# First mixer of a two-block network: the three queues in another order, pair sums on VectorE, fillers between the output products

## What is computed

```python
z = rmsnorm(h) @ w_in                    # split into hq, hf, hi, hg, cq, ckv, kr
# half A: gated recurrence, 4 heads of 128, in chunks of 64 tokens
log_f, k = gate(hf); q = silu(hq); b = cumsum(log_f)
att = (q_t * exp(b_t - b_s) * k_s), s <= t          # inside a chunk
o   = att @ v + (q * exp(b)) @ S;  S' = exp(b_last) * S + (k * exp(b_last - b))^T @ v
o_a = rmsnorm(o, out_gain) * silu(hg)
# half B: latent attention, 4 heads of 128 + 64 rotated
q, kv = rmsnorm(cq) @ w_q_up, rmsnorm(ckv) @ w_kv_up
o_b = softmax(rope(rmsnorm(q)) @ rope(rmsnorm(k))^T) @ v   # block causal
h  += concat(o_a, o_b) @ w_out
```

## Time and profile before

| | us |
|---|---|
| median of three runs | 1336.14 |
| the profiled execution | 1339.7 |
| its span | 1337.9 |
| first mixer, intra(0) to the first product of wout | 56.05 to 216.92 |
| TensorE busy in the span | 1290.3 (96%) |
| VectorE, ScalarE busy | 894.0 (67%), 740.4 (55%) |
| mean granted TensorE clock | 0.966 |

### The profile page before, as it was taken

How to read it: one execution, slowest core, us unless ns; L and a number is a source line. 1 busy time by engine, 2 the same in 40 slices (tenths; PEclk the granted TensorE clock), 3 DMA queues, 4 the chain that set the end, 5 groups by cost and what they waited for, 6 DMA issues and landing times.

```text
span 1337.9 us, 24797 instructions
## 1 busy us (share of the span) xinstructions
PE 1290.3 (96%) x10371; PEld 1264.1 (94%) x10371; DVE 894.0 (67%) x1546; ACT 740.4 (55%) x1263; POOL 7.6 (1%) x17
## 2 busy tenths in 40 slices
PE   5898999999999999999999999999999989999997
PEld 5888887999999999999999999999999989999997
DVE  4753537576544666644486599985687857999655
ACT  5742324466444566533455566664676766666544
POOL 1000000000000000000000000000000000000000
PEclk9988678999999999999999999999989999999998
DMA  6221104365555265555365365656355333666630
GB/s 243 85 84 43 48 17 142 113 218 175 189 172 165 94 209 183 187 188 183 121 226 188 104 203 192 191 186 219 99 158 191 127 126 127 194 200 191 205 127 32
DMA packets 58891, 205.54 MB, mean 154 GB/s; under 512 B 6515, under 2 KB 8860, under 8 KB 58524
## 3 DMA queue, kind: packets, MB, share of 16 engines
q1 hardware_dynamic: 57104, 201.77, 46.3%
q10 hardware_dynamic: 1676, 2.19, 0.5%
HBM read 202.87 MB, written 1.06 MB: 152 GB/s over the span
## 4 chain that ended last, share of the span: by engine, by line
PE 90%; DVE 4%; ACT 4%; DMA 1%; issue 1%; ACTq 0%; DVEq 0%
PE PS L361 69%; PE PS L409 7%; PE PS L372 2%; PE PS L447 2%; PE PS L630 1%; PE PS L392 1%; ACT WH L339 1%; DVE WL L346 1%; PE PS L496 1%; PE PS L2229 1%; ACT EE L2387 1%; PE PS L668 0%; ACT L508 0%; PE PS L667 0%; PE PS L826 0%
## 5 line engine op out<-in xcount | busy, mean ns | idle before, releaser
L346 DVE TENSOR_TENSOR WL<-RAW,WH 128x1024 fp32r<-128x1024 f32 (+2 forms) x385 | 460.3, 1201 | 219.9 <-ACT WH L339 219.3
L339 ACT ACTIVATE WH<-RAW 128x1024 fp32r<-128x1024 f32 (+2 forms) x385 | 392.3, 1038 | 235.5 <-PE PS L361 201.5
L361 PE MATMUL PS<-UH,WH 128*128 128x256 f32 (+2 forms) x1576 | 451.5, 286 | 14.3 <-DVE WL L346 7.6
L361 PE MATMUL PS<-UL,WH 128*128 128x256 f32 (+2 forms) x1576 | 451.1, 286 | 0.0
L361 PE MATMUL PS<-UH,WL 128*128 128x256 f32 (+2 forms) x1576 | 451.1, 286 | 0.0
L361 PEld LDWEIGHTS PS<-UH,WH 128*128 128x128 f32 (+1 forms) x1576 | 301.6, 191 | 16.1 <-DVE WL L346 8.4
L361 PEld LDWEIGHTS PS<-UH,WL 128*128 128x128 f32 (+1 forms) x1576 | 301.8, 191 | 0.0
L361 PEld LDWEIGHTS PS<-UL,WH 128*128 128x128 f32 (+1 forms) x1576 | 300.3, 191 | 0.0
L361 PE MATMUL PS<-HL,WH 128*128 128x272 f32 (+1 forms) x512 | 145.8, 285 | 0.0
L361 PE MATMUL PS<-HH,WH 128*128 128x272 f32 (+1 forms) x512 | 145.7, 285 | 0.0
L361 PE MATMUL PS<-HH,WL 128*128 128x272 f32 (+1 forms) x512 | 145.4, 284 | 0.0
(11 more groups left out here) (390 smaller groups left out, 1988.3 us busy)
## 6 DMA issues: line engine op xcount, KB each, us to landing
RAW<-wpack SPq DMA_DIRECT2D x363, 512.0 KB, 4.2
RAW<-wpack SPq DMA_DIRECT2D x16, 384.0 KB, 3.5
RAW<-wpack SPq DMA_DIRECT2D x6, 256.0 KB, 2.7
X<-xin SPq DMA_DIRECT2D x1, 1088.0 KB, 5.1
C<-cst SPq DMA_DIRECT2D x1, 1072.0 KB, 10.1
HB<-bias_rows ACTq DMA_DIRECT2D x1, 1024.0 KB, 5.3
out<-X SPq DMA_DIRECT2D x4, 256.0 KB, 2.3
VF<-cst ACTq DMA_DIRECT2D x1, 512.0 KB, 4.2
```

What stands on the lines that cost most here:

```text
L339: a.e.activation(WH[n % NH][:, 0:w], RAW[n % NR][:, 0:w], ACT.Copy).then_inc(*a.mark("wh", n))
L346: v.e.tensor_tensor(WL[n % NH][:, 0:w], RAW[n % NR][:, 0:w], WH[n % NH][:, 0:w].bitcast(f32), ALU.subtract).then_inc(*v.mark("wl", n))
L361: ins = t.e.matmul(o, part(n, hw, kw, a, b), x(kx), start=first and not i and not p, stop=last and i == len(kcs) - 1 and p == 2)
```

## The change

Every edit is in the first mixer and the norm ahead of it. On TensorE levels, sums, spreads, values, rotations and projections stand in another order; the recurrence's output products stand ahead of the scores, two fillers before them and two between heads. VectorE adds pairs of squares (latent_pairs, head_pairs) and TensorE sums one array in place of two. VectorE does operands ahead of the eviction of a level, exponents two levels ahead, and KD, QE earlier; ScalarE's list follows. Left out of the diff: the first norm's root sums take 16 columns in place of 128 for the 16-token block, with RS set to 1 by GpSimd at the start; two memsets of zeros go; queries on ScalarE is cut in two, its second part being query_rest.

```diff
...
 def latent_sums():
     b = banks.take(t, ("lat",), ("lm",))
+    t.wait_ge("lsum")
     for x in range(2):
-        for m in range(2):
-            t.wait_ge("lsq", 2 * x + m)
         for i, a in enumerate(WIDE):
-            for m in range(2):
-                ins = t.e.matmul(PS[:, b, 3 * x + i:3 * x + i + 1], LSQ[:, 2 * x + m, a:a + 128],
-                                 ONE[:, 0:1], start=m == 0, stop=m == 1)
+            ins = t.e.matmul(PS[:, b, 3 * x + i:3 * x + i + 1], LSQ[:, 2 * x, a:a + 128], ONE[:, 0:1],
+                             start=True, stop=True)
     ins.then_inc(*t.mark("mix", "lat"))
-def head_sums_by_token(key, sq, rsq, freed):
-    t.wait_ge("zero", 8)
-    t.wait_ge("hsq", key, 0)
-    t.wait_ge("hsq", key, 1)
+def head_sums_by_token(key, sq, freed):
+    t.wait_ge("hsum", key)
     b = banks.take(t, ("hs", key), freed)
     for i, a in enumerate(WIDE):
         for hh in range(4):
-            o = PS[:, b, 4 * i + hh:4 * i + hh + 1]
-            t.e.matmul(o, sq(hh)[:, a:a + 128], ONE[:, 0:1], start=True, stop=False)
-            ins = t.e.matmul(o, rsq(hh)[:, a:a + 128], ONE[:, 0:1], start=False, stop=True)
+            ins = t.e.matmul(PS[:, b, 4 * i + hh:4 * i + hh + 1], sq[:, hh, a:a + 128], ONE[:, 0:1],
+                             start=True, stop=True)
     ins.then_inc(*t.mark("mix", "hs", key))
...
 level(0)
 project("kr", (0,), "ev")
+level(1)
 latent_sums()
-level(1)
 up("qup", 0, [(0, 0), (1, 1)], 128, ("qn",))
+level(2)
 up("qup", 1, [(0, 0), (1, 1)], 64, ("gr", "q"))
-level(2)
+level(3)
+spread_columns("l", lambda i, hh, n: LAT[0:n, 1, i:i + 1], ("rkv",), 1)
 up("kvup", 0, [(0, 2), (1, 3)], 128, ("kn",))
-spread_columns("l", lambda i, hh, n: LAT[0:n, 1, i:i + 1], ("rkv",), 1)
+level(4)
 value_up()
-level(3)
+level(5)
+head_sums_by_token("q", QSQ, ("qm",))
 values(0)
-head_sums_by_token("q", lambda hh: QSQ[:, hh, :], lambda hh: TMA[:, hh, :], ("qm",))
-level(4)
-values(1)
-head_sums_by_token("k", lambda hh: KSQ[:, hh, :], lambda hh: ACC[1][:, 1, :], ("hroot", "k"))
-level(5)
+head_sums_by_token("k", KSQ, ("hroot", "k"))
 rotate("q", QR, 4)
-project("hg", range(2), "ev")
 rotate("k", KR, 1)
-spread_columns("k", lambda i, hh, n: KSC[0:n, i, hh:hh + 1], ("rope", "k"), 4)
 for i, (a, z) in enumerate(TILES):
     t.wait_ge("kdec")
...
     for hh in range(4):
         ins = t.e.transpose(PS[0:z - a, b, 128 * hh:128 * hh + 128], KD[:, hh, a:z], ID[:, :])
     ins.then_inc(*t.mark("mix", "kt", i))
-project("hg", range(2, 4), "ev")
+values(1)
+spread_columns("k", lambda i, hh, n: KSC[0:n, i, hh:hh + 1], ("rope", "k"), 4)
 for ch in range(4):
     chunk(ch)
-for i in (2, 1, 0):
-    scores(i)
+project("hg", range(2), "ev")
+keep_going(t, 2)
 ob = banks.take(t, ("out",), ("outa",), 4)
 t.wait_ge("att", 6)
 t.wait_ge("qe")
...
             s0 = a + 64 * cc
             ins = t.e.matmul(PS[:, b, s0:s0 + 64], STS[2 * i + cc][:, vs], QE[:, hh, s0:s0 + 64],
                              start=False, stop=cc == 1)
+    if hh < 3:
+        keep_going(t, 2, done=("ones",))
 ins.then_inc(*t.mark("mix", "out"))
+scores(2)
+scores(1)
+out_sums()
+scores(0)
+project("hg", range(2, 4), "ev")
+out_rows()
 turn(0)
 turn(1)
-out_sums()
 attend(0)
 turn(2)
 attend(1)
 turn(3)
-out_rows()
 attend(2)
 attend(3)
...
+exponents(2)
 latent(1, 1)
 act_split(a, 15)
-exponents(2)
+exponents(3)
...
+act_split(a, 16)
...
+exponents(4)
+queries()
 act_split(a, 17)
-exponents(3)
-queries()
+exponents(5)
+query_rest()
 a.wait_ge("mix", "hr", "l")
...
-exponents(4)
+a.wait_ge("kn")
+a.wait_ge("lm")
+a.e.activation(KSQ[:, :, :], KN[:, :, :], ACT.Square).then_inc(*a.mark("hsq", "k", 0))
 value_rows()
-a.wait_ge("kn")
...
-act_split(a, 21)
-exponents(5)
-values(0)
-act_split(a, 23)
...
 a.wait_ge("decay")
 a.e.activation(E[:, :, :], E[:, :, :], ACT.Exp).then_inc(*a.mark("edec"))
 a.e.activation(EL[:, :, 0:1], B[:, :, 15:16], ACT.Exp)
 a.e.activation(EL[:, :, 1:5], B[:, :, 79:T:64], ACT.Exp).then_inc(*a.mark("el"))
+act_split(a, 21)
 a.wait_ge("kdec")
 a.e.activation(E[:, :, :], B[:, :, :], ACT.Exp).then_inc(*a.mark("eb"))
+a.wait_ge("qm")
+a.e.activation(QSC[:, :, :], QSC[:, :, :], ACT.Sqrt, bias=EPS[:, 0:1], scale=1.0 / 192).then_inc(
+    *a.mark("hroot", "q"))
+act_split(a, 22)
+values(0)
+act_split(a, 23)
+a.wait_ge("mix", "hs", "k")
+a.e.activation(KSC[:, :, :], PS[:, banks.at["hs", "k"], 0:12].rearrange("p (i h) -> p i h", h=4), ACT.Sqrt,
+               bias=EPS[:, 0:1], scale=1.0 / 192).then_inc(*a.mark("hroot", "k"))
...
+act_split(a, 25)
+values(1)
 act_split(a, 27)
-for h in range(4):
+for h in range(2):
     a.wait_ge("ev", "hg", h)
     a.e.activation(HG[:, h, :], HG[:, h, :], ACT.Silu).then_inc(*a.mark("hgsilu", h))
+a.wait_ge("mix", "out")
+a.wait_ge("qe")
+ob = banks.at["out",]
+a.e.activation(E[:, :, :], PS[:, ob:ob + 4, 0:T], ACT.Square).then_inc(*a.mark("osq"))
 preload(a, ACT.Exp)
 for i in (2, 1, 0):
     m, P = TILES[i][1] - TILES[i][0], (PM, PA, PB)[i]
...
                              scale=QSC[0:m, i, hh:hh + 1],
                              accum_out=STT[0:m, i, 4 + hh:5 + hh])
     ins.then_inc(*a.mark("pexp", i))
-a.wait_ge("mix", "out")
-a.wait_ge("qe")
-ob = banks.at["out",]
-a.e.activation(E[:, :, :], PS[:, ob:ob + 4, 0:T], ACT.Square).then_inc(*a.mark("osq"))
+a.wait_ge("mix", "hs", "o")
+a.e.activation(ROOTO, PS[:, banks.at["hs", "o"], 0:T], ACT.Sqrt, bias=EPS[:, 0:1], scale=1.0 / 128).then_inc(
+    *a.mark("hroot", "o"))
+for h in range(2, 4):
+    a.wait_ge("ev", "hg", h)
+    a.e.activation(HG[:, h, :], HG[:, h, :], ACT.Silu).then_inc(*a.mark("hgsilu", h))
...
-a.wait_ge("mix", "hs", "o")
-a.e.activation(ROOTO, PS[:, banks.at["hs", "o"], 0:T], ACT.Sqrt, bias=EPS[:, 0:1], scale=1.0 / 128).then_inc(
-    *a.mark("hroot", "o"))
+a.wait_ge("onorm")
+a.e.activation(UH[:, 0:4, :], OUTA[:, :, :], ACT.Copy).then_inc(*a.mark("uh", "o", 3))
 attend(0)
 turn(2)
 attend(1)
 turn(3)
-a.wait_ge("onorm")
-a.e.activation(UH[:, 0:4, :], OUTA[:, :, :], ACT.Copy).then_inc(*a.mark("uh", "o", 3))
 attend(2)
 attend(3)
...
+def latent_pairs():
+    for m in range(4):
+        v.wait_ge("lsq", m)
+    l4 = LSQ[:, :, :].rearrange("p (x m) t -> p x m t", x=2)
+    v.e.tensor_tensor(l4[:, :, 0, :], l4[:, :, 0, :], l4[:, :, 1, :], ALU.add).then_inc(*v.mark("lsum"))
+def head_pairs(key, sq, rsq):
+    v.wait_ge("hsq", key, 0)
+    v.wait_ge(*(("hsq", "q", 1) if key == "q" else ("krsq",)))
+    v.e.tensor_tensor(sq[0:64, :, :], sq[0:64, :, :], rsq, ALU.add).then_inc(*v.mark("hsum", key))
...
-    v.wait_ge(*(("mix", "hs", "q") if key == "q" else ("rsum", "q")))
+    v.wait_ge(*(("hsum", "q") if key == "q" else ("rsum", "q")))
...
-prepare(0)
-attention(0)
+exponents(1)
+operands(0)
 latent(0, 0)
 latent(0, 1)
+attention(0)
+exponents(2)
 dve_split(v, 13)
+latent(1, 0)
+operands(1)
 attention(1)
-prepare(1)
-latent(1, 0)
+exponents(3)
 latent(1, 1)
+latent_pairs()
+dve_split(v, 14)
 key_rest()
-dve_split(v, 14)
+operands(2)
+attention(2)
 latent_means()
+exponents(4)
 dve_split(v, 15)
-attention(2)
-prepare(2)
+operands(3)
+attention(3)
 latent_roots()
-dve_split(v, 17)
+exponents(5)
+dve_split(v, 16)
+operands(4)
+attention(4)
 query_rest()
-attention(3)
-prepare(3)
-keys()
-v.wait_ge("krsq")
-v.e.tensor_scalar(KR[:, 0, :], KR[:, 0, :], g("krn", 0, 64), None, ALU.mult).then_inc(*v.mark("gr", "k"))
-dve_split(v, 19)
-query_means()
-attention(4)
-prepare(4)
-dve_split(v, 21)
-query_roots()
-attention(5)
-prepare(5)
-key_roots()
-dve_split(v, 23)
-rotated("q", QR[:, :, :], 4)
-attention(6)
-v.wait_ge("op", 5)
+v.wait_ge("op", 4)
 v.e.tensor_tensor(E[:, :, 0:16], B[:, :, 15:16].to_broadcast([128, 4, 16]), B[:, :, 0:16], ALU.subtract)
 for hh in range(4):
     v4 = (lambda z: z[:, hh, 16:T].rearrange("p (n s) -> p n s", s=64))
     ins = v.e.tensor_tensor(v4(E), v4(B)[:, :, 63:64].to_broadcast([128, 4, 64]), v4(B), ALU.subtract)
 ins.then_inc(*v.mark("decay"))
+dve_split(v, 17)
+keys()
+operands(5)
+attention(5)
+head_pairs("q", QSQ, QRSQ)
+dve_split(v, 18)
+attention(6)
+head_pairs("k", KSQ, KRSQ.unsqueeze(1).to_broadcast([64, 4, T]))
+v.e.tensor_scalar(KR[:, 0, :], KR[:, 0, :], g("krn", 0, 64), None, ALU.mult).then_inc(*v.mark("gr", "k"))
+dve_split(v, 19)
+query_means()
+v.wait_ge("edec")
+v.wait_ge("mix", "att", 0)
+v.wait_ge("op", 5)
+v.e.tensor_tensor(KD[:, :, :], K[:, :, :], E[:, :, :], ALU.mult).then_inc(*v.mark("kdec"))
+dve_split(v, 21)
+v.wait_ge("eb")
+v.e.tensor_tensor(QE[:, :, :], Q[:, :, :], E[:, :, :], ALU.mult).then_inc(*v.mark("qe"))
+query_roots()
+dve_split(v, 23)
+key_roots()
+rotated("q", QR[:, :, :], 4)
+rotated("k", KR[:, :, :], 1)
+normed()
+v.wait_ge("mix", "att", 6)
+chunk(0)
+for ch in range(1, 4):
+    chunk(ch)
+dve_split(v, 25)
 divided("hg", 0, HG)
 divided("hg", 1, HG)
-rotated("k", KR[:, :, :], 1)
-v.wait_ge("edec")
-v.wait_ge("mix", "att", 0)
-v.e.tensor_tensor(KD[:, :, :], K[:, :, :], E[:, :, :], ALU.mult).then_inc(*v.mark("kdec"))
-normed()
-dve_split(v, 25)
-v.wait_ge("eb")
```

(35 more changed lines are left out.)

32 lines of the change are left out of this document (8 added, 24 removed).

## The result

| | before | after |
|---|---|---|
| median, us | 1336.54 (4 runs, 1331.01 to 1337.06) | 1321.69 (4 runs, 1320.31 to 1322.67) |
| profiled execution, span | 1339.7, 1337.9 | 1322.67, 1320.9 |
| first product of wout starts | 216.92 | 197.18 |
| clock from 63.43 to that product | 0.77 | 0.82 |

The ratio is 0.9897, 95% interval 0.987 to 0.9925: faster by 1.0%, 14.9 us. The forecast was 1310.0 with a range of 1300 to 1321. The sign is right; the time is 11.7 us above the forecast and outside the range.

A forecast was written before the change was run, and what follows sets the result against it. TensorE was taken to bound the stretch from 63.43 us to wout, losing 18.0 us idle and 71 us at half clock. Stage by stage wout moved from 216.9 to 190.8, saving 26.1: 1336.1 − 26.1 = 1310.0 us, range 1300 to 1321.

The forecast's parts named there:

- 63.43 to kvup0: From the end of level(0)'s products: kr's wait gone, a new 3.2 us wait for QR, kvup0 at 86.0 instead of 89.43.
- kvup0 to the output: From 86.0 to 147.5: kvup0 at half clock (5.4), values(0) 8.5 plus 1.0, spread of k 4.5, chunks 3.7.
- The output: The recurrence's output products behind hg 0 and 1: full clock, 6.6 us, with six fillers 7.4, against 13.25 before.
- Scores and sums: Behind a new 2.4 us wait for OUTA: scores(2) 6.5, scores(1) 3.0, output sums 3.0, scores(0) 0.7 us.
- Four attends and two turns at the pace of before 7.5: Behind a 2.2 us wait for onorm, ahead of wout: these items take 7.5 us; UH, UL, WL 2.0 more.
- Everything behind it unchanged, about 1121 us: From the start of wout to the end: nothing changes, about 1121 us.
- B: Rival: the recurrence's output stays at half clock, 7.4 us longer, total 1317; chance 0.16.
- C: Rival: the clock stays up wherever TensorE is not long idle, total 1300; chance 0.13.
- D: Rival: the order only moves the waits, idle and half clock stay at 18 and 61 us, total 1330.5; chance 0.09.
- the sum by kinds: Cross-check of the saving: sums 6.7 less, fillers 1.1 more, idle 18.0 to 13.1, half clock 14: 24.5 us.
- E: Rival: slower, the fallen clock never rises from 86 to 181 us, some 52 us more, total 1362; chance 0.04.
- it falls everywhere and the output stays at half: Upper end of the terms, clock falling at all new waits: +7.4, values +2, the rest +4, total 1323.

The follow-up runs named there:

- third experiment: The changed kernel without its 8 fillers, the two ahead of the output and the six within it: 1317.87 us, ratio 0.9879.
- the version with fillers: The changed kernel with query_rest ahead of operands(4) and fillers ahead of KD's transposes, scores(2), attend(0) and wout: 1302.58 us, ratio 0.9763.

## Why the prediction was wrong

By its own steps, from the start of intra(0) (56.05 before, 54.63 after) to the start of wout: forecast a saving of 26.1 us, measured 160.87 − 142.55 = 18.3.

- **63.43 to kvup0: right.** kr without a wait and at full clock (3.14 us), 12 passes for the latents (1.47), a wait of 3.5 for QR, kvup0 at 84.96 (forecast 86.0; it would be 86.4 if intra(0) hadn't started 1.4 us earlier). The earlier start is not the change's doing: the changed kernel's own two traces differ by 1.0 us in it.
- **kvup0 to the output: right within 3.3 us, to the good.** kvup0 took 4.6 instead of 5.4, values(0) 8.6 at 1.00 where 1.0 was added for a fall, spread 3.8, chunks 3.3. The output started 88.2 us behind intra(0), forecast 91.45.
- **The output: right.** Full clock, 8.1 us for 7.4. The step "it follows 6 us of projections, so I take full clock" held; the term for the fillers was small, but the trace without them shows them as pure cost.
- **Scores and sums: mis-sized.** Forecast 6.5 + 3.0 + 3.0 + 0.7 = 13.2, measured 16.8. The step wrote that the clock falls again at the wait and then took the middle between full and half; it is at half throughout, 7.9 + 4.4 + 3.9.
- **"Four attends and two turns at the pace of before 7.5": the step that failed.** It priced them by the full-clock rate with a wait of 2.2 us written right ahead of them. They took 13.8. The forecast's own rule for kvup0 and for scores(2), a wait of this length is followed by half clock, was left out for the wait for onorm, and again for the one ahead of wout. With UH, UL and WL this is 15.95 us against 9.5. With 16 fillers in the wait the same items took 7.6 us, so it is the clock, and not the hand-offs between the engines, that the step had wrong.
- **"Everything behind it unchanged, about 1121 us" was off by 2.7 us:** 1123.7. The step took the diff's end for the change's end. The rotation of the banks carries the change on through all later layers, which the text did not look for. The longer wait for M, 1.6 us, is shown to come from it. Another 1.9 us lie behind that wait, where the changed kernel runs at half clock for a while and the kernel before does not (255.0 us to the end, against 253.1); their cause is open, and 0.8 came back on the way there.
- **Median and trace.** The spans differ by 17.0 us, the medians by 14.9: the profiled execution of before was 3 us above its median, that of the changed kernel 1.

Sum: 26.1 − 18.3 = 7.8, less 1.4 for the earlier start of intra(0), plus 2.7 and 2.1, is 11.2 of the 11.7 missed. The rest is the median of before, 1336.5 with a fourth run where the forecast had 1336.1.

**The rivals.** B falls (third experiment). C, the clock stays up, falls as a forecast for this kernel (2 × 0.18 × 133.75 = 48 us at half), but it is what the fillers make true, and its 1300 is near the 1302.3 that was then measured. D, only the waits move, got 0.09 and comes closest in sense: beside the pair sums the order brings 1 us, not to be told from nothing. The 1330.5 that it gave was wrong because of the sum by kinds below. E doesn't occur: the clock came back each time.

**The sum by kinds** had 6.7 us for the sums at full rate and called the half clock behind them the order's. Against the kernel before in the same series the pair sums alone brought 13 to 14: about half of their worth is work behind them that no longer runs at half clock.

**The range.** The text worked out 1323 for "it falls everywhere and the output stays at half" and closed the range at 1321 on B alone. But falls at the late waits were likelier than not by its own rows: behind 1.72 us stands 0.50, and behind 2.94 us the first product of wout takes 0.59 us, where at full clock the version with fillers shows 0.39.
